# A hybrid trunk layer on one core: the short projection chunk loaded ahead of the last scale load, tokens written exact and then rounded

## What is computed

```python
mod = silu(c) @ w_mod + b_mod            # one row for each of the two kinds of token
sh1, sc1, g1, sh2, sc2, g2 = split(mod, 6)
hn = rms_norm(x, norm1_w) * (1 + sc1) + sh1
proj = hn @ w_in                         # 1024 x 2832, split into q, k, v, gates, qm, km, vm, om
```

## Time and profile before

| | us |
|---|---|
| runs shown, without profile | 632.5, 632.64, 634.05 |
| their median | 632.64 |
| the profiled execution, its own time | 633.4 |
| span of its trace | 632.0 |
| TensorE busy | 579.1 |
| VectorE busy | 211.5 |
| ScalarE busy | 167.8 |
| DMA queue of SyncE, share of 16 engines' span | 94.7% |

### The profile page before, as it was taken

How to read it: one execution, slowest core, us unless ns; L and a number is a source line. 1 busy time by engine, 2 the same in 40 slices (tenths; PEclk the granted TensorE clock), 3 DMA queues, 4 the chain that set the end, 5 groups by cost and what they waited for, 6 DMA issues and landing times.

```text
span 632.0 us, 9859 instructions
## 1 busy us (share of the span) xinstructions
PE 579.1 (92%) x3936; PEld 360.2 (57%) x3936; DVE 211.5 (33%) x476; ACT 167.8 (27%) x308; POOL 31.8 (5%) x77
## 2 busy tenths in 40 slices
PE   0799999999999999969999999697999999996987
PEld 0478787788867575724545555255545454544354
DVE  0297778687822222012121212120121212122123
ACT  3182637672622121101212121210212121212011
POOL 1340210011100000000000000000000000000001
PEclk9989999999999999979999999899999999999889
DMA  9999699989999999999999999999999999999996
GB/s 355 412 383 327 201 392 398 426 305 423 399 377 368 404 422 416 426 424 429 423 424 427 425 425 425 421 420 421 429 424 425 428 424 427 421 426 424 420 404 229
DMA packets 30354, 252.48 MB, mean 399 GB/s; under 512 B 4296, under 2 KB 4944, under 8 KB 8800
## 3 DMA queue, kind: packets, MB, share of 16 engines
q1 hardware_dynamic: 28080, 247.29, 94.7%
q0 software_dynamic: 1840, 4.21, 2.1%
q10 hardware_dynamic: 384, 0.30, 0.1%
HBM read 250.06 MB, written 1.72 MB: 398 GB/s over the span
## 4 chain that ended last, share of the span: by engine, by line
PE 67%; DMA 24%; SPq 4%; DVE 3%; issue 2%; ACT 1%; DVEq 0%
DMA ring<-in_w_gate_up 21%; PE bank L1353 17%; PE bank L1457 9%; PE bank L1372 6%; PE bank L1391 5%; PE bank L1323 5%; PE bank L912 4%; PE bank L954 3%; PE bank L962 3%; PE bank L958 3%; SPq L682 2%; DMA ring<-in_w_down 2%; DMA xt<-in_x_sample 1%; PE bank L1075 1%; SPq L716 1%
## 5 line engine op out<-in xcount | busy, mean ns | idle before, releaser
L1353 PE MATMUL bank<-ring,xe 128*64 128x512 f32 (+1 forms) x640 | 133.0, 626 | 17.8 <-DMA ring<-in_w_gate_up 17.8
L1353 PEld LDWEIGHTS bank<-ring,xe 128*64 128x64 f32 (+1 forms) x640 | 45.9, 137 | 102.5 <-issue 102.5
L2439 DVE TENSOR_TENSOR act_e<-bank,sil 128x256 f32<-128x256 f32 x26 | 11.0, 425 | 172.6 <-ACT sil L1851 172.6
L1866 ACT ACTIVATE yhi<-bank,gslot 128x512 fp32r<-128x512 f32 x50 | 34.4, 687 | 109.0 <-PE bank L1457 109.0
L2453 DVE SCALAR_TENSOR_TENSOR ylo<-bank,gslot,yhi 128x512 fp32r<-128x512 f32 x50 | 37.5, 750 | 76.4 <-ACT yhi L1866 76.4
L1851 ACT ACTIVATE sil<-bank 128x256 f32<-128x256 f32 x26 | 10.0, 384 | 194.5 <-PE bank L1353 136.0
L1372 PE MATMUL bank<-ring,xe 128*32 128x256 f32 (+1 forms) x624 | 55.9, 393 | 6.2 <-DMA ring<-in_w_gate_up 6.0
L1323 PE MATMUL bank<-pone,hhi 128*128 128x256 f32 x192 | 47.9, 288 | 0.0
L1323 PE MATMUL bank<-pone,hlo 128*128 128x256 f32 x192 | 46.9, 282 | 0.0
L1372 PEld LDWEIGHTS bank<-ring,xe 128*32 128x32 f32 (+1 forms) x624 | 33.9, 121 | 20.6 <-issue 11.0
L1391 PE MATMUL bank<-yhi,ptone 128*128 128x512 f32 x100 | 42.3, 423 | 0.0
(11 more groups left out here) (393 smaller groups left out, 832.5 us busy)
## 6 DMA issues: line engine op xcount, KB each, us to landing
ring<-in_w_gate_up SPq DMA_DIRECT2D x40, 2048.0 KB, 22.3
ring<-in_w_gate_up SPq DMA_DIRECT2D x35, 1024.0 KB, 12.3
ring<-in_w_mod SPq DMA_DIRECT2D x12, 2048.0 KB, 11.3
ring<-in_w_down SPq DMA_DIRECT2D x17, 1024.0 KB, 12.3
xn<-in_w_down SPq DMA_DIRECT2D x11, 1024.0 KB, 17.9
spare<-in_w_down SPq DMA_DIRECT2D x11, 1024.0 KB, 13.7
gb<-in_w_down SPq DMA_DIRECT2D x11, 1024.0 KB, 15.7
ring<-in_w_in SPq DMA_DIRECT2D x5, 2048.0 KB, 14.7
```

The source lines that it names most:

```text
L1353: ins = mm(bank[6][j * w:(j + 1) * w, :], xe[:, k, slots], weights[:, k, :, :], start=(k == 0), stop=(k == KD - 1))
L1866: A(yhi[:, n, :], bank[4 + n][:, :], ACT.Copy, scale=gslot[:, par:par + 1]).then_inc(y_hi, 1)
```

## The change

- The second A1 chunk and the short projection chunk change places in the order of the loads. The A1 chunk, now behind it, is loaded as two DMAs of half its columns, with a semaphore of its own for the first, and TensorE's matmuls on it wait for either half by itself.
- TensorE no longer begins with `transpose_tokens(0)`. All tokens are transposed, with A0's columns in front, between the two halves of `mod_rows("A1")`.
- Rounding the short chunk (both halves) and subtracting for its rest now stand in front of the A1 row copy on VectorE, and in front of the wait for `ab_ready` on ScalarE.
- Each bank of tokens is read once, exact into `hT`, by ScalarE for xT0 and xT1 and by VectorE for xT2 and xT3; the same engine then rounds `hT` into `xhi` by one copy of 4 x 128 columns.
- Chunk 0's rounding is done by ScalarE alone.
- GpSimd's small loads wait for the A1 chunk's last half as before.

```diff
-        for what in ("A0", "A1", 1, 0, 2, 3, "g1", 4, "m0", 5, "m1", "g2"):
+        for what in ("A0", "A0", "A1", 1, "A1", 0, 2, 3, "g1", "g1", 4, "m0", "m0", 5, "m1", "m1", "g2", "g2"):
...
+        HALF_LOAD = mod_chunks["A1"][1]
...
             def load_chunk(i):
                 if i >= 4:
                     chunk_free(i - 4)
+                if i == HALF_LOAD:
+                    v = slice(0, CH // 2), slice(CH // 2, CH)
+                    sp.dma_start(chunk(i)[:, v[0]], loads[i][:, v[0]]).then_inc(half_loaded, 16)
+                    sp.dma_start(chunk(i)[:, v[1]], loads[i][:, v[1]]).then_inc(chunk_loaded[i % 4], 16)
+                    return
...
-            def mod_rows(name):
+            def mod_rows(name, between=None):
...
+                    if a == 1 and between:
+                        between()
+                    halves = i == HALF_LOAD
+                    if halves:
+                        pe.wait_ge(half_loaded, 16)
+                    else:
+                        chunk_ready(i)
...
+                        if halves and k == CT // 2:
+                            chunk_ready(i)
...
-            transpose_tokens(0)
             mod_rows("A0")
-            complete("cA0", mod_columns("A0", "cA0"))
-            mod_rows("A1")
+
+            def columns_and_tokens():
+
+                complete("cA0", mod_columns("A0", "cA0"))
+                for s in range(NST):
+                    transpose_tokens(s)
+
+            mod_rows("A1", columns_and_tokens)
             complete("cA1", mod_columns("A1", "cA1"))
-            transpose_tokens(1)
...
             rows_out("A0")
-            act.wait_ge(ab_ready, 1)
...
-            token_upper(0)
             act.wait_ge(chunk_loaded[proj_chunk[1] % 4], need[proj_chunk[1]])
             A(proj_upper(1)[:, 0:4, :], proj_weights(1)[:, 0:4, :], ACT.Copy).then_inc(w_upper, 1)
-            token_upper(1)
-            for b in (0, 1, 3):
-                token_exact(b)
+            act.wait_ge(ab_ready, 1)
+
+            def first_tokens(s):
+
+                tok = slice(s * P, s * P + P)
+                ps = product(act, f"xT{s}")
+                for k in range(4):
+                    ins = A(hT[:, k, tok], ps[:, k * P:k * P + P], ACT.Identity,
+                            bias=modc[:, 0, k, s:s + 1], scale=acol[:, k, s:s + 1])
+                ins.then_inc(x_exact[0], 1)
+                act.wait_ge(x_exact[0], s + 1)
+                act.sem_inc(drained[where[f"xT{s}"]], 1)
+                A(xhi[:, 0:4, tok], hT[:, 0:4, tok], ACT.Copy).then_inc(x_upper[0], 1)
+
+            first_tokens(0)
+            first_tokens(1)
...
-            A(proj_upper(0)[:, 0:6, :], proj_weights(0)[:, 0:6, :], ACT.Copy).then_inc(w_upper, 1)
+            A(proj_upper(0), proj_weights(0), ACT.Copy).then_inc(w_upper, 1)
...
             mod_vector("cA0", 0, 0, modc)
+            dve.wait_ge(chunk_loaded[proj_chunk[1] % 4], need[proj_chunk[1]])
+            V.tensor_copy(proj_upper(1)[:, 4:8, :], proj_weights(1)[:, 4:8, :]).then_inc(w_upper_part, 1)
+            dve.wait_ge(w_upper_part, 1)
+            rest_of_weights(dve, 1)
             ps = product(dve, "rA1")
...
+            def last_tokens(s):
+
+                tok = slice(s * P, s * P + P)
+                ps = product(dve, f"xT{s + 2}")
+                for k in range(4, 8):
+                    ins = V.tensor_scalar(hT[:, k, tok], ps[:, (k - 4) * P:(k - 3) * P],
                                           acol[:, k, s:s + 1], modc[:, 0, k, s:s + 1], ALU.mult, ALU.add)
-                drain(f"xT{b}", ins)
+                ins.then_inc(x_exact[1], 1)
+                dve.wait_ge(x_exact[1], s + 1)
+                V.sem_inc(drained[where[f"xT{s + 2}"]], 1)
+                V.tensor_copy(xhi[:, 4:8, tok], hT[:, 4:8, tok]).then_inc(x_upper[1], 1)
+
+            last_tokens(0)
+            last_tokens(1)
...
-            token_full(2)
             token_rest(0)
             token_rest(1)
-            dve.wait_ge(chunk_loaded[proj_chunk[0] % 4], need[proj_chunk[0]])
-            V.tensor_copy(proj_upper(0)[:, 6:8, :], proj_weights(0)[:, 6:8, :]).then_inc(w_upper_part, 1)
```

More of the change, by code:

```diff
@@ L361, in build @@
         c_exp, c_silu = sem("c_exp"), sem("c_silu")
-        x_upper = [sem(f"x_upper{b}") for b in range(4)]
+        x_upper = [sem(f"x_upper{a}") for a in range(2)]
+        x_exact = [sem(f"x_exact{a}") for a in range(2)]
+        half_loaded = sem("half_loaded")
         x_rest, w_upper, w_rest = sem("x_rest"), sem("w_upper"), sem("w_rest")
         w_upper_part = sem("w_upper_part")
-        first_rest, g2_biased = sem("first_rest"), sem("g2_biased")
+        g2_biased = sem("g2_biased")
         wout_upper, wout_rest = sem("wout_upper"), sem("wout_rest")
@@ L422, in build @@
         loads = []
-        def mod_loads(q):
-            return [t["w_mod"][q, a] for a in range(2)]
-        mod_first = {}
+        mod_chunks = {name: [] for name in MODS}
         proj_chunk = {}
@@ L429, in build @@
         used = 0
-        for what in ("A0", "A1", 1, 0, 2, 3, "g1", 4, "m0", 5, "m1", "g2"):
+        for what in ("A0", "A0", "A1", 1, "A1", 0, 2, 3, "g1", "g1", 4, "m0", "m0", 5, "m1", "m1", "g2", "g2"):
             if isinstance(what, str):
[L432 to L435, removed]
+                half = len(mod_chunks[what])
+                mod_chunks[what].append(len(loads))
+                loads.append(t["w_mod"][MODS.index(what), half])
+                used += half == 0
+                last_use.append(f"r{what}" if half else used)
             else:
@@ L968, in project @@
                     for s in range(NST):
-                        for b in (s, s + 2):
-                            pe.wait_ge(x_upper[b], 1)
+                        for a in range(2):
+                            pe.wait_ge(x_upper[a], s + 1)
                         upper_upper(s)
-                    pe.wait_ge(first_rest, 1)
+                    pe.wait_ge(w_upper_part, 2)
                     for s in range(NST):
@@ L1644, in _ @@
             rows_out("A0")
-            act.wait_ge(ab_ready, 1)
[L1647 to L1665, removed]
-                drain(f"xT{b}", ins)
-            def evacuated_once(b):
-                act.wait_ge(drained[where[f"xT{b}"]], drains[f"xT{b}"] - 1)
-            token_upper(0)
             act.wait_ge(chunk_loaded[proj_chunk[1] % 4], need[proj_chunk[1]])
             A(proj_upper(1)[:, 0:4, :], proj_weights(1)[:, 0:4, :], ACT.Copy).then_inc(w_upper, 1)
-            token_upper(1)
-            for b in (0, 1, 3):
-                token_exact(b)
+            act.wait_ge(ab_ready, 1)
[11 more added lines that the diff above has]
+            first_tokens(1)
             def proj_out(c):
@@ L1765, in upper_wout @@
                 act.wait_ge(wout_loaded[part // 2], 16)
-                act.wait_ge(chunk_used, last_use[mod_first["m1"]])
+                act.wait_ge(chunk_used, last_use[mod_chunks["m1"][0]])
                 if part == 2:
@@ L2006, in _ @@
             mod_scale("cA1", 0, modc, acol, ab_ready)
-            def token_upper(b):
-                s = b % 2
-                ps = product(dve, f"xT{b}")
-                for i in range(4):
-                    ins = V.tensor_scalar(xhi[:, 4 + i, s * P:s * P + P], ps[:, i * P:i * P + P],
-                                          acol[:, 4 + i, s:s + 1], modc[:, 0, 4 + i, s:s + 1], ALU.mult, ALU.add)
-                drain(f"xT{b}", ins)
-                dve.wait_ge(drained[where[f"xT{b}"]], drains[f"xT{b}"] - 1)
-                V.sem_inc(x_upper[b], 1)
@@ L2034, in token_rest @@
+            last_tokens(0)
+            last_tokens(1)
             def token_rest(s):
-                for b in (s, s + 2):
-                    evacuated(dve, f"xT{b}")
+                for a in range(2):
+                    dve.wait_ge(x_upper[a], s + 1)
                 V.tensor_tensor(xlo[:, :, s * P:s * P + P], hT[:, :, s * P:s * P + P],
                                 xhi[:, :, s * P:s * P + P].bitcast(F32), ALU.subtract).then_inc(x_rest, 1)
-            dve.wait_ge(w_upper_part, 1)
-            rest_of_weights(dve, 1)
```

28 lines of the change are left out of this document (6 added, 22 removed).

## The result

| | before | changed |
|---|---|---|
| median of 20 runs each, us | 633.75 (632.38 to 634.92) | 636.25 (633.85 to 638.02) |
| profiled execution | 633.4, span 632.0 | 636.88, span 635.6 |

The ratio is 1.0040, interval 1.0031 to 1.0048: slower by 2.5 us, where +0.75 was forecast. The absolute time misses by 2.85: 1.75 of it is the change, and 1.1 that the kernel before reads 633.75 over 20 runs, not the 632.64 of the three runs shown, on which the forecast stood.

What follows compares the result with a forecast made beforehand. TensorE's opening chain, then the expert weight stream, was taken to bound the kernel. Row copy +1.55 and chain from the scale -0.8 gave +0.75 us on 632.64, so 633.4 us, range 631.2 to 635.8.

Steps and rivals of the forecast that it cites:

- moves the stream and the end by the same amount: Whole kernel: what TensorE's chain wins or loses in the opening shifts slot releases, expert weight stream and end equally.
- The row copy: Opening: the A1 row copy starts at about 30.1 in place of 28.57 us, +1.55 us.
- the landing: Opening: the A1 chunk, behind the short one, lands whole at about 29.17 in place of 26.57 us, 2.60 later.
- rival B: Loads before A1's last half: each pays its own fixed cost, two more give +3.0 us, end 636.4; chance 0.03.
- the chain from the scale: Scale ready to second projection chunk: 10.45 us in place of 11.24, -0.8 us, with 1.2 GHz lasting 3.1 us.
- rival A: First projection: the gap between token blocks keeps TensorE's clock low, end 635.2 or 637.3 us; chance 0.16.
- a granted clock of 0.5 after 37 us: First projection: the sign that would show the forecast wrong by the clock staying low.
- The copies of the tokens: Opening: rounding 512 token columns out of SBUF in one copy takes 0.61 us, bounds 0.44 and 1.11.
- every cover: Opening: ScalarE's rounding of the second chunk, chunk 3's later load and the moved transposes stay hidden, at no cost.
- rival D: End: the opening's shift is absorbed, 632.6 us; sign, the end moving otherwise than the second projection's start; chance 0.11.

Runs made afterwards that it cites:

- `order_back`: The changed kernel with the short chunk loaded behind the last A1 chunk again (still in halves) and rounded behind the first token block; ratio 1.0016, median 634.57 us.
- `order_alone`: The kernel before with only the new load order and the A1 chunk in two halves; ratio 1.0072, median 638.15 us.
- `a1_whole`: The changed kernel with the last A1 chunk loaded as one 2 MB DMA; ratio 1.0043, median 636.39 us.
- `warm_after`: The changed kernel with 12 added matmuls on constants in TensorE's idle time before the first projection; ratio 1.0021, median 634.81 us.
- `inert`: The kernel before with 9 added matmuls at the start of TensorE's program, where it waits for the first loads anyway; ratio 1.0003, median 633.50 us.
- `tokens_alone`: The kernel before with only the single reading of the token banks and ScalarE's rounding of chunk 0; ratio 1.0014, median 634.19 us.
- `back_again`: `order_back` run once more, unchanged, against the kernel before; ratio 1.0021.
- `halves_alone`: The kernel before with the last A1 chunk in two DMAs and all token transposes between A1's halves, old load order; ratio 1.0015, median 634.76 us.
- `delay`: The kernel before with 19 added matmuls in front of the first projection; ratio 1.0018, twelve executions at 633.04 to 633.74 or 635.79 to 637.05 us.
- `after_again`: The changed kernel traced once more, unchanged; opening +1.44 us.

## Why the prediction was wrong

**What bounds it, right up to 259 us.** TensorE waited for nothing that the prediction had not named, and the opening's shift was carried to 259 us within 0.25 us in every version (+2.2 in the changed kernel, -0.65 in `order_back`) but `order_alone` (+3.9 at 53 us, +4.45 from 191 on). That it "moves the stream and the end by the same amount" failed behind 259 us; see "The rest".

**The row copy, +1.55 forecast, +2.26 measured.** This is the step that failed in every trace. It is the landing first: 29.17 forecast, 29.69 to 29.93 measured. The bytes put in front were counted at 428 GB/s, 2.60 us; they cost 3.12. Why more, no run shows. The other 0.2 is the half's matmuls: 29.69 to 30.83 is 1.14, not 0.93, for the term took the pitch of the records and left the last one's way to the copy out. A fixed cost for the second DMA, the half of rival B, is out by `a1_whole`. The Trainium skill, "DMA: Bandwidth & Descriptors", Rules for kernel authors, has the fixed setup cost overlap with compute when a DMA is issued early; it doesn't speak of loads queued behind each other, and here those landed at 29.69 both ways.

**The clock, -0.8 forecast for the chain from the scale, +0.1 measured in the first trace.** In that execution this step failed by 0.9. In both repeats it held: 10.35 us in place of 11.24 is -0.9. The prediction let the 1.2 GHz level last 3.1 us from the projection's start; it lasted 5.9, 3.7 and 3.7. So rival A (chance 0.16) came true in one trace of three: there the projection's second group cost 3.06 - 2.18 = 0.9 more. Its sign, a granted clock of 0.5 after 37 us, stands in all three, but its reason doesn't hold: `warm_after` has the gap between the two token blocks (0.71 us) and stays at 1.00. That the forecast held in the other two is partly luck, as its paces per matmul, 0.139 and 0.227 us, are 0.126 (41.58 to 43.60 for 16) and 0.246 (34.74 to 38.68) in the trace, and the errors nearly cancel. At 2.4 GHz throughout the chain is 41.90 - 32.31 = 9.59 us (`warm_after`): the change does shorten it, by 1.65, and the clock takes back 0.8 or all of it.

When is the stretch long? Over the thirteen traces with one at the first projection, all but `order_alone` (10.2 us) fall in two groups. It lasts 3.4 us where the clock fell at most 0.3 us ahead of the projection's first matmul, or behind it (the three traces of the kernel before, `inert`, `tokens_alone`, `a1_whole`), and 6.8 where it fell 0.9 to 3.2 us ahead (the three of the changed kernel, `order_back`, `back_again`, `halves_alone`). The number of idle pieces doesn't order them: `order_back` has one wait of 3.85 us behind steady work and 6.8, `a1_whole` waits of 2.35 and 3.04 us and 3.4. Whether the change brings the early fall or only allows it, three traces of each kernel can't tell.

The copies of the tokens (0.63 measured, 0.61 forecast) and every cover (rounding by ScalarE done at 40.15, chunk 3, transposes behind slack) held.

**The rest, nothing forecast, about 0.9 us measured.** Averaged over three traces of each kernel the row copy is +2.20, the chain -0.58, so the opening +1.62; the median is 2.5 over. Of the 1.75 us that the change missed by, 0.65 is thus the row copy, 0.2 the chain, and 0.9 lies behind the opening, where the prediction put nothing. The end did move otherwise than the second projection's start, the sign that the prediction gave for rival D, but to the slower side, not absorbed. The traced executions show more of it: their spans (635.6, 635.2, 635.1, before 632.0, 631.8, 631.7) part by 3.5. Between 259 and 293 us, where the DMA share is 1.01, the loads fall back by another 0.7 to 1.9 in the three traces of the changed kernel and by nothing (0.0 to -0.1) in those of the kernel before. But `delay` moves by -0.9 to +1.5 there in four executions of one kernel. Over all twenty traces it goes with the 1.2 GHz stretch that begins between 274 and 280 us: where that ends 1.0 to 1.8 earlier than in the kernel before, the opening's shift taken off, the loads gain 0.4 to 1.0; where it ends 1.1 to 2.6 later, they lose 0.3 to 1.9; in between they move by -0.2 to +0.7. That is a correlation, with no run that moves the stretch alone. `tokens_alone`, with no opening shift, also reads 1.0014. What in the change moves that stretch, and which wait at the end turns this into time, stays open.

**The base.** The other 1.1 us of the absolute miss is the base: three runs gave 632.64 where twenty give 633.75. The profiled execution's time (634.15 as a forecast) would have been 0.75 nearer.

## What to carry to other kernels

A transfer moved ahead of the one that the chain waits for costs its bytes, and here 0.5 us over; what is made ready by it must be on the chain too, and by more. Where a reordering leaves TensorE a wait ahead of a long run of matmuls, ask when the clock falls in it: here executions of one kernel differed by 0.9 us for that alone, and the first trace alone makes the clock look like the main loss. An opening's microsecond was passed on in full only to where the stream of weights sets the pace; for half a per cent, compare medians of ten or more executions, not profiles.

## What the runs showed of the hardware

- The granted clock's low stretches were 3.4, 6.8 or, three times, 10.2 us long, and began at times that differ by 2.2 us between executions of one kernel. The Trainium skill, "TensorE: Matmul & The Clock Gate", HAM oscillation, puts the danger in long idle gaps; here the clock fell 2.1 us into a wait (before, at 32.4; changed, at 33.8), and in `after_again` at 31.6 with waits of 1.55 and 0.55 us the last behind it.
- One 2 MB load in two DMAs landed as early as in one (29.69), with another queued in front.
- TensorE stopped for 0.4 to 3.6 us in straight code with its data there, at a place that moved record for record with the code ahead of it, with the DMA share at 1.02 to 1.04 in the four traces of `delay`; each of the eight stops ended 1.2 to 1.5 us after a packet of the instruction queue.
